# Sum of squares of a recurrence head as two rounded products, two key tiles later

## The chip, the cores and the metric

The kernel runs on one core of a Trainium2 chip. The metric is the device time of one execution in microseconds (us). Engines are called as the profile calls them: PE (TensorE matmul), PEld (its weight load), DVE (VectorE), ACT (ScalarE), POOL (GpSimd) and SP (SyncE, which here issues the loads of weights).

## The reference

Two blocks in a row work on x of 512 tokens and 1024 features: a gated MLP and a chunked attention, then a block with two branches, one of which is a gated linear recurrence with 8 heads of 128 channels. The change touches what follows the recurrence of a head: its output is divided by the root of its mean square over the 128 channels, and gated.

```python
    o = hgrn2_recurrence(q, k, v, log_f).astype(dt)
    o = rms_norm_2(o, hg_norm_g)          # per token, over the 128 channels of a head
    o = o * jax.nn.silu(hz).reshape(B, S, HG_HEADS, HG_DIM)
```

with `rms_norm_2(x, g) = x * rsqrt(mean(x*x) + 1e-6) * g`.

## The kernel before

Activations lie with features on the 128 partitions and the 512 tokens along the free axis. A product whose result must be near float32 is done as three products of rounded halves (`mm3`, lines 462 to 464): a tensor is cut into a high part (ACT, type fp32r) and the remainder (DVE or POOL, fp32r), and PE runs high by high, low by high, high by low. Weights come in 512 KB slabs: SP loads a slab into `raw` (L440), ACT rounds it (`whi`, L973, called `cut()`), POOL subtracts (`wlo`, L452), and PE's `slab()` multiplies it in 8 key tiles k = 0 to 7 with three products of 512 columns each.

The engines' programs are written out by hand and run in that order; semaphores (`Steps`, one count per named step) are the only link. The recurrence is a software pipeline over rounds r = 0 to 7. In round r PE runs the slabs `hq` r, `hf` r, `mz` r-2 and `hz` r, and between their key tiles it puts small products of head s = r-1: in slab `hq` (`hg_scores`, L737) the transposes of the keys after k = 3, the diagonal score blocks after k = 4 and 5, the cross blocks after k = 6 and 7; in slab `hf` (`hg_updates`, L750) the state updates after k = 3, 4 and 5, which wait for DVE's `ktlo` (L1773); in slab `hz` (`hg_outputs`, L761) the outputs, into bank 3. Slab `hq` also carries, after k = 2, the step that is changed, for head u = r-2: `hg_square` (L732) multiplies the all-ones matrix by the squared output `ho`, which gives each token's sum of squares on all partitions in bank 6. The square of head 6 stands in slab `dn` 0 in the same manner; that of head 7 stands alone behind slab `dn` 3 (L815).

ACT's round r (L1260 to 1299) is: `hg_root(u)` (square L1188, wait for the product, Ln L1190, Exp L1192), a cut, the two gates of `z`, the high part `kthi` of the transposed keys (L1209), a cut, the high part of the scores (L1216), Silu of the query (L1226), a cut that waits until PE has done slab `hf` r, then sigmoid and logarithm of the forget gate, the state halves, a cut, the exponentials (`hg_decays`) and four high parts (`hg_halves`, the last of them L1257). DVE's round is `hg_finish(u)` (L1760: norm, gate, `yhi`, `ylo`; it begins by waiting for ACT's Exp), `hg_stage(s)` (L1771) and `hg_project(r)` (L1797 to L1847), which ends with the low parts `klo`, `kolo`, `qlo` and `qblo` (L1839 to L1846). So PE in round r squares head r-2 when DVE is at the end of `hg_project(r-1)` or past it.

Of the kernel before, what the change touches and what calls it, by code (L numbers as in the profile page):

```python
# [22 lines left out]
F32 = mybir.dt.float32  # L23
F32R = mybir.dt.float32r
U32 = mybir.dt.uint32
ALU = mybir.AluOpType
ACT = mybir.ActivationFunctionType

P = 128
S = 512  # L30
# [8 lines left out]
HH = 8  # L39
# [93 lines left out]
def build(nc, xt, w, vecs, ws, bs, relx, consts, masks_hg, masks_ml, xs, rel_tab, tk, out):  # L133
    ctx = ExitStack()
    with ctx:
        def sb(name, shape, dt, where=ctx):
            return where.enter_context(nc.sbuf_tensor(name, shape, dt))

        def sem(name):
            return ctx.enter_context(nc.semaphore(name))  # L140
# [4 lines left out]
        ident, ones, eps = cst[:, 0:P], cst[:, P:2 * P], cst[:, 2 * P:2 * P + 1]  # L145
# [12 lines left out]
        yhi = sb("yhi", [P, AH, S], F32R)  # L158
# [5 lines left out]
        ylo = sb("ylo", [P, AH, S], F32R)  # L164
# [48 lines left out]
        with ExitStack() as scope:  # L213
            he = sb("he", [P, S], F32, scope)
            hf = sb("hf", [P, S], F32, scope)
            hk = sb("hk", [P, S], F32, scope)
            hb = sb("hb", [P, S], F32, scope)
            hd = sb("hd", [P, S], F32, scope)
            heb = sb("heb", [P, S], F32, scope)
            hen = sb("hen", [P, S], F32, scope)  # L220
            hq = sb("hq", [P, S], F32, scope)
            hx = sb("hx", [P, TT, 12], F32, scope)
            hfac = sb("hfac", [P, TT, 12], F32, scope)
            hqx = sb("hqx", [P, TT, HX], F32, scope)
            hqxs = [sb(n, [P, TT, HX], F32R, scope) for n in ("hqxhi", "hqxlo")]
            hqb = sb("hqb", [P, TT - 1, P], F32, scope)
            hqbs = [sb(n, [P, 2, TT - 1, P], F32R, scope) for n in ("hqbhi", "hqblo")]
            hks = [sb(n, [P, S], F32R, scope) for n in ("hkhi", "hklo")]
            hkos = [sb(n, [P, S], F32R, scope) for n in ("hkohi", "hkolo")]
            hkb = sb("hkb", [P, TT - 1, P], F32, scope)  # L230
            hkts = [sb(n, [P, TT - 1, P], F32R, scope) for n in ("hkthi", "hktlo")]
            hs = sb("hs", [P, S], F32, scope)
            hss = [sb(n, [P, S], F32R, scope) for n in ("hshi", "hslo")]
            hst = sb("hst", [P, TT - 1, P], F32, scope)
            hsts = [sb(n, [P, TT - 1, P], F32R, scope) for n in ("hsthi", "hstlo")]
            hz = sb("hz", [P, 2, S], F32, scope)
            ho = sb("ho", [P, 2, S], F32, scope)
            hm = sb("hm", [P, S + P + CROSS], F32, scope)
# [32 lines left out]
        bank = [banks[:, i * S:(i + 1) * S] for i in range(8)]  # L271
# [17 lines left out]
        def steps(name, names, rounds=1, prime=0):  # L289
            s = Steps(sem(name), names, rounds, prime)  # L290
            all_steps.append(s)
            return s
# [13 lines left out]
        def norm_steps(name, n, cut, squares=False):  # L306
            v = ["mean", "inv"]
            for t in range(n + 1):
                v += [f"full{t}"] if t < n else []
                if t >= 1:  # L310
# [25 lines left out]
                    for n in ("affine", "gate", "y", "yhi", "ylo")], 8, prime=1)  # L336
# [20 lines left out]
        hpV = steps("hp_dve", ["k", "b", "rest", "t12", "t03", "pairs", "mid", "three0", "three1", "four", "qin", "kin",  # L357
                               "kout", "two", "three", "kb", "qb", "klo", "kolo", "qlo", "qblo"], HH)
# [1 line left out]
        htA = steps("ht_act", ["z", "kthi", "shi", "sthi"], HH)  # L360
        htV = steps("ht_dve", ["ktlo", "diag", "near", "mid", "far", "slo", "st1", "st2", "st3", "stlo"], HH)
        hoP = steps("ho_pe", ["ms"], HH)
        hoA = steps("ho_act", ["sq", "ln", "root"], HH)
        hoV = steps("ho_dve", ["norm", "y", "yhi", "ylo"], HH)
        mzA = steps("mz_act", ["z"], HH)
        hzV = steps("hz_dve", ["zero", "one0", "one1"])
        dnP = steps("dn_pe", ["tok", "wide"])
        dnA = steps("dn_act", numbered("sq", QL + KL) + ["kp", "root", "wide0", "wide1"] + numbered("hi", QL + KL))
        dnV = steps("dn_dve", ["q1", "q2", "k1"] + ["turn"] + numbered("cross", 4) + ["sum", "mean", "inv", "kplo", "diag"]
# [31 lines left out]
        def f32(ap):  # L401
            return ap.bitcast(F32)
# [54 lines left out]
        def _(pe):  # L457
# [243 lines left out]
            def hg_keys(s):  # L701
                pe.wait_ge(hpV.sem, hpV.at("kb", s))
                if s >= 1:
                    pe.wait_ge(htV.sem, htV.at("st3", s - 1))
                for t in range(TT - 1):
                    last = nc.tensor.transpose(bank[4][:, t * P:(t + 1) * P], hkb[:, t, :], ident)
                last.then_inc(htP.did("kt"), 1)

            def hg_diagonal(s, t):
                if t == 0:  # L710
                    pe.wait_ge(hpV.sem, hpV.at("qlo", s))
                    if s >= 1:
                        pe.wait_ge(htV.sem, htV.at("diag", s - 1))
                cols = slice(t * P, (t + 1) * P)
                last = mm3(bank[5][:, cols], [u[:, cols] for u in hks], [u[:, t, 0:P] for u in hqxs], True, True)
                if t == TT - 1:
                    last.then_inc(htP.did("diag"), 1)

            def hg_cross(s, t):
                if t == 0:  # L720
                    if s >= 1:
                        pe.wait_ge(htV.sem, htV.at("far", s - 1))
                        pe.wait_ge(hoA.sem, hoA.at("ln", s - 1))
                if t == 2 and s >= 2:
                    pe.wait_ge(mzA.sem, mzA.at("z", s - 2))
                cols = slice(t * P, (t + 1) * P)
                last = mm3(banks[:, 6 * S + t * 2 * P:6 * S + t * 2 * P + CROSS], [u[:, cols] for u in hkos],
                           [u[:, t, HC:HX] for u in hqxs], True, True)
                if t == TT - 1:
                    last.then_inc(htP.did("cross"), 1)  # L730

            def hg_square(u):  # L732
                pe.wait_ge(hoA.sem, hoA.at("sq", u))
                pe.wait_ge(htV.sem, htV.at("far", u))
                nc.tensor.matmul(bank[6], ones, ho[:, 0, :], start=True, stop=True).then_inc(hoP.did("ms"), 1)  # L735

            def hg_scores(r, k):  # L737
                s, u = r - 1, r - 2
                if k == 2 and u >= 0:
                    hg_square(u)  # L740
                if k == 3:
                    hg_keys(s)
                if k in (4, 5):
                    hg_diagonal(s, 2 * (k - 4))
                    hg_diagonal(s, 2 * (k - 4) + 1)
                if k in (6, 7):
                    hg_cross(s, 2 * (k - 6))
                    hg_cross(s, 2 * (k - 6) + 1)
# [31 lines left out]
            for r in range(HH):  # L780
                s, u = r - 1, r - 2
# [111 lines left out]
            for g, t in enumerate((0, QL)):  # L893
                for b in range(TT):
                    tok = nc.tensor.matmul(bank[6][:, g * TT + b:g * TT + b + 1], dsq[:, t, b * P:(b + 1) * P], ones[:, 0:1],
                                           start=True, stop=True)
# [61 lines left out]
        def _(act):  # L958
# [57 lines left out]
            for r in range(4):  # L1016
                for j in range(4):
                    if r or j:
                        cut()
                    if r in (1, 2):  # L1020
                        k = 4 * (r - 1) + j
# [162 lines left out]
            def hg_root(u):  # L1184
                if u >= 1:
                    act.wait_ge(hoV.sem, hoV.at("ylo", u - 1))
                act.wait_ge(htP.sem, htP.at("o", u))
                nc.scalar.activation(ho[:, 0, :], bank[3], ACT.Square).then_inc(hoA.did("sq"), 1)  # L1188
                act.wait_ge(hoP.sem, hoP.at("ms", u))
                nc.scalar.activation(ho[:, 1, :], bank[6], ACT.Ln, bias=eps, scale=1.0 / P).then_inc(hoA.did("ln"), 1)  # L1190
                act.wait_ge(hoA.sem, hoA.at("ln", u))
                nc.scalar.activation(ho[:, 1, :], ho[:, 1, :], ACT.Exp, scale=-0.5).then_inc(hoA.did("root"), 1)  # L1192
# [67 lines left out]
            for r in range(HH + 1):  # L1260
                s, u = r - 1, r - 2
                if u >= 0:
                    hg_root(u)
# [156 lines left out]
        def _(dve):  # L1420
            V = nc.vector
# [36 lines left out]
            def cols(name, n, first=0):  # L1458
                return [vec[:, VEC[name] + first + t:VEC[name] + first + t + 1] for t in range(n)]
# [298 lines left out]
                return ap.to_broadcast([P, *shape])  # L1758

            def hg_finish(u):  # L1760
                dve.wait_ge(hoA.sem, hoA.at("root", u))
                V.scalar_tensor_tensor(ho[:, 0, :], bank[3], cols("hg_g", 1)[0], ho[:, 1, :], ALU.mult,
                                       ALU.mult).then_inc(hoV.did("norm"), 1)
                dve.wait_ge(hoV.sem, hoV.at("norm", u))
                V.tensor_tensor(ho[:, 0, :], ho[:, 0, :], hz[:, u % 2, :], ALU.mult).then_inc(hoV.did("y"), 1)
                dve.wait_ge(hoV.sem, hoV.at("y", u))
                V.tensor_copy(yhi[:, u, :], ho[:, 0, :]).then_inc(hoV.did("yhi"), 1)
                dve.wait_ge(hoV.sem, hoV.at("yhi", u))
                V.tensor_tensor(ylo[:, u, :], ho[:, 0, :], f32(yhi[:, u, :]), ALU.subtract).then_inc(hoV.did("ylo"), 1)
# [79 lines left out]
            V.memset(hs[:, :], 0.0).then_inc(hzV.did("zero"), 1)  # L1849
            V.memset(hfac[:, :, 0:1], 1.0).then_inc(hzV.did("one0"), 1)  # L1850
            V.memset(hfac[:, :, 11:12], 1.0).then_inc(hzV.did("one1"), 1)
            dve.wait_ge(st_x, 16)
            dve.wait_ge(ld_hm, 16)
            dve.wait_ge(hzV.sem, hzV.all())
# [254 lines left out]
```

## Time and profile before

| | us |
|---|---|
| three runs | 1358.9, 1359.68, 1362.27 (median 1359.68) |
| the profiled execution: its own time | 1360.59 |
| its span, first to last instruction | 1358.8 |
| PE busy in the span | 1306.7 (96%) |
| DVE, ACT, POOL busy | 719.0, 646.5, 493.8 |

The profile gives start and duration of each instruction. PE's instructions are pipelined, so a product of 512 columns is shown 0.39 us long while the next one starts 0.23 us after it: PE's work is read from the distance between starts and not from durations. The rounds of the recurrence lie between 700 and 1010 us and repeat every 29.6 us.

### The profile page before, as it was taken

What the parts mean: (1) busy time and instruction counts of PE and PEld (TensorE: products, weight loads), DVE (VectorE), ACT (ScalarE), POOL (GpSimd) and SP (SyncE); (2) the same over time, 40 slices, a digit from 0 to 9 for tenths busy, and PEclk for the clock granted to TensorE, in tenths of its full rate; (3) what the DMA queues carried; (4) which work ended last, traced back from release to release, by engine and by line L of the source; (5) the groups of instructions that cost most, each with busy time, mean ns of one, the idle gap of its engine ahead of it and who ended that gap; (6) DMA issues with size and microseconds to landing.
All of it is one profiled execution on the core that took longest, in us unless ns stands there. A gap on an engine that the chain in (4) does not pass through costs nothing.

```text
span 1358.8 us, 16181 instructions
## 1 busy us (share of the span) xinstructions
PE 1306.7 (96%) x6346; PEld 1084.1 (80%) x6346; DVE 719.0 (53%) x1256; ACT 646.5 (48%) x957; POOL 493.8 (36%) x206
## 2 busy tenths in 40 slices
PE   6999999999999999999998899999999999999985
PEld 4787888888888888888876788888887888888864
DVE  6464646552236465554766376766626546642325
ACT  4344444542334556464435466656546545542211
POOL 2454344434444323322334433333333333234430
PEclk9999999999999999999999999999999999999998
DMA  5542232334232322322224322222223222234421
GB/s 222 187 139 87 92 99 82 93 101 156 94 108 93 92 78 80 104 62 72 68 82 147 109 63 62 72 78 68 78 93 96 73 80 87 88 103 153 131 62 62
DMA packets 42155, 132.31 MB, mean 97 GB/s; under 512 B 6944, under 2 KB 9696, under 8 KB 41440
## 3 DMA queue, kind: packets, MB, share of 16 engines
q1 hardware_dynamic: 36704, 116.41, 27.2%
q10 hardware_dynamic: 5376, 14.87, 3.1%
q8 instruction: 50, 0.82, 0.2%
q14 instruction: 25, 0.20, 0.0%
HBM read 124.97 MB, written 10.49 MB: 100 GB/s over the span
## 4 chain that ended last, share of the span: by engine, by line
PE 78%; DVE 11%; ACT 6%; issue 2%; DMA 1%; POOL 1%; ACTq 0%; DVEq 0%; SPq 0%
PE banks L462 24%; PE banks L464 24%; PE banks L463 24%; DVE hd L1805 1%; PE banks L624 1%; PE banks L613 1%; DVE naccb L1705 1%; ACT L1232 1%; POOL wlo L452 1%; DVE hb L1802 1%; ACT L1233 1%; PE banks L856 1%; DVE acc L1478 1%; PE banks L735 1%; DMA x_kept<-x 1%
## 5 line engine op out<-in xcount | busy, mean ns | idle before, releaser
L452 POOL TENSOR_TENSOR wlo<-raw,whi 128x1024 fp32r<-128x1024 f32 (+2 forms) x202 | 493.6, 2446 | 829.8 <-ACT whi L973 829.8
L462 PE MATMUL banks<-hhi,whi 128*128 128x512 f32 x752 | 304.7, 405 | 4.5 <-POOL wlo L452 3.3
L973 ACT ACTIVATE whi<-raw 128x1024 fp32r<-128x1024 f32 (+2 forms) x202 | 210.2, 1041 | 201.8 <-PE banks L464 149.4
L464 PE MATMUL banks<-hlo,whi 128*128 128x512 f32 x752 | 294.3, 391 | 0.0
L463 PE MATMUL banks<-hhi,wlo 128*128 128x512 f32 x752 | 294.1, 391 | 0.0
L462 PE MATMUL banks<-yhi,whi 128*128 128x512 f32 x448 | 176.5, 394 | 0.0
L464 PE MATMUL banks<-ylo,whi 128*128 128x512 f32 x448 | 174.6, 390 | 0.0
L463 PE MATMUL banks<-yhi,wlo 128*128 128x512 f32 x448 | 174.4, 389 | 0.0
L462 PEld LDWEIGHTS banks<-hhi,whi 128*128 128x128 f32 x752 | 142.0, 189 | 33.2 <-issue 5.6
L464 PEld LDWEIGHTS banks<-hlo,whi 128*128 128x128 f32 x752 | 141.6, 188 | 30.6
L463 PEld LDWEIGHTS banks<-hhi,wlo 128*128 128x128 f32 x752 | 142.0, 189 | 26.8 <-issue 1.9
L462 PE MATMUL banks<-whi,yhi 128*128 128x512 f32 x224 | 90.4, 404 | 18.0 <-DVE ylo L1470 12.3
L462 PEld LDWEIGHTS banks<-yhi,whi 128*128 128x128 f32 x448 | 84.1, 188 | 20.8 <-issue 3.0
L464 PEld LDWEIGHTS banks<-ylo,whi 128*128 128x128 f32 x448 | 84.1, 188 | 17.9
L463 PEld LDWEIGHTS banks<-yhi,wlo 128*128 128x128 f32 x448 | 84.2, 188 | 17.0
L463 PE MATMUL banks<-whi,ylo 128*128 128x512 f32 x224 | 88.6, 396 | 0.0
L464 PE MATMUL banks<-wlo,yhi 128*128 128x512 f32 x224 | 88.4, 395 | 0.0
L462 PEld LDWEIGHTS banks<-whi,yhi 128*128 128x128 f32 x224 | 42.8, 191 | 29.0 <-POOL wlo L452 19.2
L1107 ACT ACTIVATE sc<-sc,sm 128x128 f32<-128x128 f32 (+1 forms) x64 | 35.1, 553 | 47.2 <-DVE sm L1664 47.2
L463 PEld LDWEIGHTS banks<-whi,ylo 128*128 128x128 f32 x224 | 42.9, 192 | 9.5 <-issue 0.7
L464 PEld LDWEIGHTS banks<-wlo,yhi 128*128 128x128 f32 x224 | 42.9, 192 | 9.1
L1557 DVE SCALAR_TENSOR_TENSOR mt<-banks,vec,bb 128x512 f32<-128x512 f32 x16 | 12.0, 751 | 70.0 <-PE banks L554 70.0
(359 smaller groups left out, 2116.1 us busy)
## 6 DMA issues: line engine op xcount, KB each, us to landing
raw<-w SPq DMA_DIRECT2D x194, 512.0 KB, 3.5
rel_tab<-relx ACTq DMA_DIRECT2D x1, 4096.0 KB, 21.4
tab<-rel_tab SPq DMA_DIRECT2D x16, 224.0 KB, 3.5
x<-xt SPq DMA_DIRECT2D x4, 512.0 KB, 6.5
x<-xt ACTq DMA_DIRECT2D x1, 2048.0 KB, 8.1
x_kept<-x ACTq DMA_DIRECT2D x1, 2048.0 KB, 7.3
parts_kept<-mcg SPq DMA_DIRECT2D x8, 256.0 KB, 4.4
mgt<-parts_kept SPq DMA_DIRECT2D x8, 256.0 KB, 3.9
```

Of the source, the lines that this page charges most:

```text
L452: nc.gpsimd.tensor_tensor(wlo[:, n % 4, 0:width], raw[:, n % 2, 0:width], f32(whi[:, n % 4, 0:width]), ALU.subtract).then_inc(lo_done, 1)
L462: nc.tensor.matmul(dst, a[0], b[0], start=first, stop=False)
L463: nc.tensor.matmul(dst, a[1], b[0], start=False, stop=False)
L464: return nc.tensor.matmul(dst, a[0], b[1], start=False, stop=last)
L613: done = nc.tensor.matmul(banks[:, c:c + QW[t]], a[rows, t * P:(t + 1) * P], b[rows, 0:QW[t]], start=first, stop=last)
L624: last = nc.tensor.transpose(banks[:, c:c + P], sc[:, q, of:of + P], ident)
L735: nc.tensor.matmul(bank[6], ones, ho[:, 0, :], start=True, stop=True).then_inc(hoP.did("ms"), 1)
L856: last = nc.tensor.transpose(bank[b][:, c:c + P], msc[:, QO[t] + k * P:QO[t] + (k + 1) * P], ident)
L973: nc.scalar.activation(whi[:, n % 4, 0:width], raw[:, n % 2, 0:width], ACT.Copy).then_inc(hi_done, 1)
L1107: e = nc.scalar.activation(row, row, ACT.Exp, bias=sm[:, q, 1, t:t + 1], accum_out=sm[:, q, 2, t:t + 1])
L1232: nc.scalar.activation(he[:, :], bank[0], ACT.Sigmoid).then_inc(hpA.did("f"), 1)
L1233: act.preload_act_table_set("natural_log_exp_and_others")
```

## The change

The ones matrix is copied once to a rounded tile `hones`. ACT, right behind the square, writes its high part `hsqhi`; DVE subtracts and writes the low part `hsqlo` at the head of `hg_finish(u)`; PE multiplies `hones` by both parts, in fp32r, and does so after key tile 4 instead of 2, ahead of the diagonal blocks. `hsqhi` has the place of `hq`, `hsqlo` that of `heb`, in the buffer.

```diff
-            heb = sb("heb", [P, S], F32, scope)
+            with ExitStack() as place:
+                heb = sb("heb", [P, S], F32, place)
+            hsqlo = sb("hsqlo", [P, S], F32R, scope)
...
-            hq = sb("hq", [P, S], F32, scope)
+            with ExitStack() as place:
+                hq = sb("hq", [P, S], F32, place)
+            hsqhi = sb("hsqhi", [P, S], F32R, scope)
+            hones = sb("hones", [P, P], F32R, scope)
...
             def hg_square(u):
-                pe.wait_ge(hoA.sem, hoA.at("sq", u))
+                pe.wait_ge(hoV.sem, hoV.at("sqlo", u))
                 pe.wait_ge(htV.sem, htV.at("far", u))
-                nc.tensor.matmul(bank[6], ones, ho[:, 0, :], start=True, stop=True).then_inc(hoP.did("ms"), 1)
+                nc.tensor.matmul(bank[6], hones[:, :], hsqhi[:, :], start=True, stop=False)
+                nc.tensor.matmul(bank[6], hones[:, :], hsqlo[:, :], start=False, stop=True).then_inc(hoP.did("ms"), 1)
...
-                if k == 2 and u >= 0:
+                if k == 4 and u >= 0:
                     hg_square(u)
...
                 nc.scalar.activation(ho[:, 0, :], bank[3], ACT.Square).then_inc(hoA.did("sq"), 1)
+                act.wait_ge(hoA.sem, hoA.at("sq", u))
+                act.wait_ge(hpV.sem, hpV.at("qin", min(u + 1, HH - 1)))
+                nc.scalar.activation(hsqhi[:, :], ho[:, 0, :], ACT.Copy).then_inc(hoA.did("sqhi"), 1)
                 act.wait_ge(hoP.sem, hoP.at("ms", u))
...
             def hg_finish(u):
+                dve.wait_ge(hoA.sem, hoA.at("sqhi", u))
+                V.tensor_tensor(hsqlo[:, :], ho[:, 0, :], f32(hsqhi[:, :]), ALU.subtract).then_inc(hoV.did("sqlo"), 1)
                 dve.wait_ge(hoA.sem, hoA.at("root", u))
...
             V.memset(hfac[:, :, 11:12], 1.0).then_inc(hzV.did("one1"), 1)
+            V.tensor_copy(hones[:, :], ones).then_inc(hzV.did("ones"), 1)
```

## Rows read from the trace of the kernel before

**Rows 1.** The page: busy time of the engines, share of the span, instructions (part 1)

```profile
PE 1306.7 (96%) x6346; PEld 1084.1 (80%) x6346; DVE 719.0 (53%) x1256; ACT 646.5 (48%) x957; POOL 493.8 (36%) x206
```

**Rows 2.** PE's waits, 785 to 1000 us: engine, line, releaser, total us, times, longest

```profile
PE banks L735 <- ACT ho L1188: 1.2, 6, 0.4
```

**Rows 3.** Timeline of PE around one square: start, duration (us), engine, line, operation, tiles

```profile
844.38 0.39 PE L464 MATMUL banks<-hlo,whi 128*128 128x512 f32 x1
844.91 1.12 PE L735 MATMUL banks<-ho,cst 128*128 128x512 f32 x2
...
846.10 0.39 PE L463 MATMUL banks<-hhi,wlo 128*128 128x512 f32 x1
...
847.59 0.23 PE L462 MATMUL banks<-hqxhi,hkhi 128*128 128x128 f32 x1
```

**Rows 4.** Timeline of DVE in the same stretch

```profile
843.26 0.55 DVE L1835 TENSOR_TENSOR hqb<-hqx,hfac 128x384 f32<-128x384 f32 x1
843.73 0.69 DVE L1839 TENSOR_TENSOR hklo<-hen,hkhi 128x512 fp32r<-128x512 f32 x1
...
845.93 0.56 DVE L1846 TENSOR_TENSOR hqblo<-hqb,hqbhi 128x384 fp32r<-128x384 f32 x1
```

**Rows 5.** Timeline of ACT in the same stretch and behind it

```profile
844.28 0.58 ACT L1188 ACTIVATE ho<-banks 128x512 f32<-128x512 f32 x1
846.07 0.69 ACT L1190 ACTIVATE ho<-banks,cst 128x512 f32<-128x512 f32 x1 [1.22 <-PE banks L735]
...
850.66 0.49 ACT L1209 ACTIVATE hkthi<-banks 128x384 fp32r<-128x384 f32 x1
852.21 1.06 ACT L973 ACTIVATE whi<-raw 128x1024 fp32r<-128x1024 f32 x1 [1.05 <-PE banks L464]
```

**Rows 6.** Timeline of PE around the square of head 7, which waits for nothing

```profile
996.17 1.02 PE L735 MATMUL banks<-ho,cst 128*128 128x512 f32 x2
...
997.27 0.40 PE L463 MATMUL banks<-hhi,wlo 128*128 128x512 f32 x1
```

**Rows 7.** Timeline of PE: rounded products of 512 columns behind a wait

```profile
44.95 0.50 PE L462 MATMUL banks<-whi,yhi 128*128 128x512 f32 x1 [3.02 <-POOL wlo L452]
45.29 0.40 PE L463 MATMUL banks<-whi,ylo 128*128 128x512 f32 x1
45.53 0.40 PE L464 MATMUL banks<-wlo,yhi 128*128 128x512 f32 x1
```

**Rows 8.** Timeline, one product of PE that waits for DVE

```profile
777.79 0.56 DVE L1794 TENSOR_TENSOR hstlo<-hst,hsthi 128x384 fp32r<-128x384 f32 x1 [5.97 <-ACT hsthi L1220]
...
778.41 0.33 PE L462 MATMUL banks<-hqbhi,hsthi 128*128 128x128 f32 x1 [2.91 <-DVE hstlo L1794]
```

**Rows 9.** Timeline of ACT, the cut that waits for slab `hf`

```profile
859.12 1.06 ACT L973 ACTIVATE whi<-raw 128x1024 fp32r<-128x1024 f32 x1 [3.10 <-PE banks L464]
```

**Rows 10.** Timeline, DVE's `ktlo` and the state update of PE that waits for it

```profile
852.12 0.55 DVE L1773 TENSOR_TENSOR hktlo<-banks,hkthi 128x384 fp32r<-128x384 f32 x1
...
855.10 0.22 PE L462 MATMUL banks<-yhi,hkthi 128*128 128x128 f32 x1
```

**Rows 11.** Timeline of POOL, from 840 to 856 us (in brackets: idle before)

```profile
848.46 2.73 POOL L452 TENSOR_TENSOR wlo<-raw,whi 128x1024 fp32r<-128x1024 f32 x1 [9.06 <-ACT whi L973]
853.35 2.41 POOL L452 TENSOR_TENSOR wlo<-raw,whi 128x1024 fp32r<-128x1024 f32 x1 [2.16 <-ACT whi L973]
```

**Rows 12.** DVE's line 1805: count, duration in ns (min/median/max), first and last start

```profile
L1805 DVE TENSOR_TENSOR hd<-hb x8: 691/2703/2716, 738.2 to 955.8; 128x512 f32<-128x512 f32 x8
```

**Rows 13.** Timeline, a DVE subtraction from a PSUM bank beside POOL

```profile
611.88 2.37 POOL L452 TENSOR_TENSOR wlo<-raw,whi 128x1024 fp32r<-128x1024 f32 x1 [12.73 <-ACT whi L973]
612.79 0.69 DVE L1634 TENSOR_TENSOR klo<-banks,khi 128x512 fp32r<-128x512 f32 x1 [3.76 <-ACT khi L1091]
```

**Rows 14.** Timeline of DVE, its first instruction of the recurrence behind the memsets

```profile
734.90 0.68 DVE L1799 TENSOR_SCALAR hk<-he,lbn,lb 128x512 f32<-128x512 f32 x1 [10.38 <-ACT he L1232]
```

**Rows 15.** Stretch 785 to 1000: busy us (instructions) of PE, PEld, DVE, ACT, POOL; clock, DMA

```profile
785.00:1000.00 215.00, 213.63 (x1117) 178.31 (x1116) 134.83 (x229) 126.03 (x175) 74.80 (x28) 1.00 0.22 69
```

More of the change, by code:

```diff
@@ L362, in build @@
         hoP = steps("ho_pe", ["ms"], HH)
-        hoA = steps("ho_act", ["sq", "ln", "root"], HH)
-        hoV = steps("ho_dve", ["norm", "y", "yhi", "ylo"], HH)
+        hoA = steps("ho_act", ["sq", "sqhi", "ln", "root"], HH)
+        hoV = steps("ho_dve", ["sqlo", "norm", "y", "yhi", "ylo"], HH)
         mzA = steps("mz_act", ["z"], HH)
-        hzV = steps("hz_dve", ["zero", "one0", "one1"])
+        hzV = steps("hz_dve", ["zero", "one0", "one1", "ones"])
         dnP = steps("dn_pe", ["tok", "wide"])
```

## Prediction

> **What bounds the kernel now.** I read the page first: PE is busy 96% of the span, the next engine 53% [rows 1]. Between 785 and 1000 us, where all eight squares lie, PE is busy 213.6 of 215.0 us at a granted clock of 1.00 [rows 15]. So a microsecond taken off PE's own sequence there is worth one, and a wait put into it costs one. Then PE's waits: in that stretch the list has one entry, the square itself, for ACT's square [rows 2]. Its 1.2 us are too small a reading, since idle time is counted there from the modelled end of a product; from start to start, as below, the wait is longer. Last, the timelines of PE, DVE and ACT around one square, that of head 2 at 844.9 us, on which all that follows is read; the other six squares inside a slab have the same distances within some 0.02 us, but for head 0, whose wait is longer.
>
> **What a square costs today.** The last product of key tile 2 starts at 844.38 [rows 3]; at 0.23 us a product its place ends at 844.61. The square starts at 844.91, when ACT's square (844.28 + 0.58 = 844.86) is there [rows 5]: a wait of 0.30. The next slab product but one starts at 846.10, so key tile 3 begins at 846.10 - 0.23 = 845.87, and the square took 0.96 us. Key tile 3, the transposes and key tile 4 take until the first diagonal product at 847.59, which is 1.72 us. Altogether 844.61 to 847.59 is 0.30 + 0.96 + 1.72 = 2.98 us. The square of head 7 waits for nothing: 996.17 to 997.27 - 0.23 = 997.04, 0.87 us [rows 6].
>
> **What it costs after, part by part.** The wait for ACT's square goes, and PE does the same 1.72 us of tiles first. It asks for `sqlo` at 844.61 + 1.72 = 846.33.
>
> When is `sqlo` ready? ACT's new copy to `hsqhi` has the size of the high parts beside it, some 0.63 us, starts at 844.9 and is done by about 845.5. Its wait for `qin` costs nothing, since DVE has passed L1819 long before L1835 at 843.26 [rows 4]. But DVE is in order, and `sqlo` stands behind the whole of `hg_project`. Its last instruction, `qblo`, starts at 845.93; behind one of that size the next starts 0.47 us later (843.26 to 843.73), thus at 846.40, and a subtraction of 128x512 with two SBUF inputs takes 0.69: 847.09 [rows 4]. From DVE's end to PE's start it is 0.06 us (777.79 + 0.56 = 778.35, to 778.41) [rows 8]. So PE goes on at 847.15: it waits 0.82 us where it waited 0.30. Nothing but PE's own stream is queued behind this wait, and on DVE nothing: it would have waited for ACT's Exp anyway.
>
> The pair itself: the trace before has no such pair, but has rounded products of 512 columns behind a wait, 44.95 to 45.29 (0.34) and then 0.24 a product [rows 7]; with 0.23 for the second it is 0.57. The first diagonal product starts at 847.15 + 0.57 = 847.72, against 847.59. Each square inside a slab costs **0.13 us more**: the 0.39 saved in the product and the 0.30 of the old wait are taken by the new wait.
>
> Is this distance kept from round to round? DVE's `hg_project` is not paced by the squares but by the slab `hf`: ACT's cut waits 3.10 us for that slab to end [rows 9], and sigmoid, logarithm, scan, exponentials and halves follow in a fixed chain down to `qblo` (from 859.12 to one round of 29.6 us behind 845.93, at 875.5, it is 16.4 us). PE runs without a wait from `hf`'s end to the next square. So PE and DVE meet with the same distances each round, and the 0.13 us are added each time. Head 0 has the same distance from `qblo` to the diagonal, the 1.66 us from 845.93 to 847.59 [rows 3, 4], and only the waits before and after are longer there, by equal amounts.
>
> Seven squares give 7 x 0.13 = +0.9 us. The square of head 7 comes a whole slab after ACT's square, with DVE idle, so both parts are there when PE asks at 996.17: 0.46 for 0.87 [rows 6], -0.4 us. **Sum +0.5 us.**
>
> *What is moved.* Ln can start at 847.15 + 0.34 + 0.39 + 0.04 = 847.92 instead of 846.07 [rows 5], so the whole chain of Ln, Exp, a cut, `kthi`, norm, `yhi`, `ylo` and `ktlo` comes 1.85 us later. Its cover: `ktlo` ends at 852.67 and PE's update starts at 855.10 [rows 10], 2.43 us; after, 854.52 against 855.23, so 0.7 us are left. The cross blocks, which must wait for Ln to have read bank 6, start two key tiles (1.4 us) and four blocks after the first diagonal product, so behind 849.1, and Ln is done by 848.61. ACT's idle 3.10 before the cut of `hf` shrinks to about 1.25 [rows 9] and still lets the chain start on time. The cuts of this part serve slabs that PE needs a slab or more later. All this costs nothing while those gaps stand.
>
> *The copy of the ones* is one DVE instruction (smaller than the 0.69 us of a 128x512 subtraction, or up to the 2.7 of one held by POOL [rows 4, 12]) ahead of 10.38 us in which DVE is idle [rows 14]: nothing.
>
> *Bounds.* `sqlo` 0.69 to 0.75 and its start 0.47 to 0.60 behind `qblo`; the way to PE 0.05 to 0.10; the pair 0.46, as with hidden loads, to 0.67, with a first product as slow as a half of today's square behind its wait. The diagonal then comes 1.58 to 2.12 us behind 845.93, against 1.66: -0.08 to +0.46 a head, with the last head -1.0 to +2.8 us in sum. I take the middle rows, as they are of the same shapes.
>
> On contention with POOL: line 1805 takes 691 ns alone and 2703 ns at the median, when it meets POOL's subtraction [rows 12]. `hsqlo` would be exposed in the same way; POOL, though, is idle for the 9.06 us before 848.46 [rows 11], and `sqlo` lies at 846.4 to 847.1. The Trainium skill (SBUF — State Buffer, "Who interferes with whom") says that a DVE instruction with two SBUF inputs contends with a GpSimd instruction that reads SBUF, whoever is second being fully blocked. By that rule the new subtraction can be held, unlike one that reads a bank; the trace agrees in the 2.0 us of line 1805.
>
> **The rivals.**
>
> *Faster: the new wait isn't there.* If `sqlo` were ready by the time PE asks, each of seven squares would save 0.30 + 0.96 - 0.46 = 0.80, with the last 6.0 us: 1353.7. For it: this is what two more key tiles of distance look like from ACT's side alone, as `hsqhi` is ready 0.8 us before PE asks. Against it: DVE's order; it would have to finish `qblo` 0.8 us earlier, and nothing in the change shortens that chain. Each 0.1 us that the wait is shorter gives 0.7.
>
> *Slower: the later root makes `ktlo` late.* `kthi` comes at 850.66 + 1.85 and ends at 853.0, ACT's cut, which today waits for PE until 852.21, then starts behind it, and POOL's subtraction starts 1.14 later, at about 854.1, within 0.2 us of `ktlo` at 853.97 [rows 5, 10, 11]. If POOL held `ktlo` as it holds line 1805, `ktlo` would end at 854.1 + 2.4 + 0.55 = 857.05, PE would wait 1.9 us in each of seven slabs `hf`, and the time be 13 us more: 1373. Against it: `ktlo` reads a PSUM bank and one SBUF tile, and such a subtraction in the midst of POOL's takes 0.69, its usual time [rows 13]. It decides from a delay of the root of 2.43 + 0.13 us on, whatever its cause.
>
> *Slower: `sqlo` meets POOL.* 2.0 us in each of seven squares, 14 us, 1374; it needs a POOL subtraction in a gap of 9 us where there is none now.
>
> **How the numbers follow.** The sum is made against the profiled execution: 1360.59 us, span 1358.8; it lies 0.9 above the median of the three runs, inside their 1358.9 to 1362.27. +0.5 on it gives 1361.1, on the median 1360.2; I predict for the median. The forecast (a change between -1.0 and +2.8) has 0.83; faster by the missing wait 0.06; slower by `ktlo` 0.06; by `sqlo` and POOL 0.03; 0.02 is left for a gain in between. For the range: the bounds give 1358.7 to 1362.5, and medians of this kernel spread by about a microsecond beside; 1357.0 to 1363.3 leaves out the three rivals and some of the rest. What a measurement can tell from no change is 0.3%, 4.1 us, so the forecast and its bounds lie within: same 0.83, faster 0.08, slower 0.09.
>
> **What would show it.** In the profile after, for each of seven squares: the first of the pair starts 1.2 us after `qblo`'s start, PE waits for DVE's `sqlo` some 0.8 us from start to start (0.6 by the list of waits, which counts from modelled ends), the diagonal starts 1.79 us after `qblo`'s start instead of 1.66; the rounds repeat every 29.7 to 29.8 us; POOL doesn't touch `sqlo`, which takes 0.69; `ktlo` ends 0.7 us before the update, and PE's list shows no wait for it. Head 7's square takes 0.46. The prediction is wrong if `qblo` ends earlier against PE than before, if `ktlo` appears in the list, or if PE's products outside the squares change their distance.

## Result and profile after

| | before | after |
|---|---|---|
| median of six runs each (us) | 1361.41 | 1366.86 |
| ratio of the runs | | 1.0049, 95% interval 1.0036 to 1.0061 |
| span of the profiled execution | 1358.8 | 1365.8 |

The change makes the kernel slower by 0.49%, some 6.7 us by the ratio (4.9 to 8.3 by its interval; the two medians differ by 5.5); the prediction was 0.5 us slower, in a range that ended at 1363.3. The time of this kernel scatters by 3 to 4 us from run to run and more over a long series, so each experiment is compared with runs of the kernel before on the same chip. A ratio below is a kernel's time over that of the kernel before, with its 95% interval in brackets; a time in us beside it is the ratio times the kernel before.

PE's waits between 785 and 1000 us, the view of [rows 2] (engine, line, what it waited for, total us, times, longest), show two entries, neither of them the one of before:

```profile
PE banks L467 <- ACT mzg L1212: 4.2, 6, 0.7
PE banks L740 <- DVE hsqlo L1771: 4.0, 6, 0.7
```

The second was forecast. The first was not in the prediction at all. It is PE waiting for ACT's Silu of the slab `mz` (L1203 of the kernel before, written to `mzg`), which empties bank 7. It is called the gate below.

PE's timeline around the square of head 2 answers to [rows 3]; lines 467 to 469 are now the three products of `mm3`:

```profile
848.80 0.40 PE L469 MATMUL banks<-hlo,whi 128*128 128x512 f32 x1
849.86 0.50 PE L740 MATMUL banks<-hsqhi,hones 128*128 128x512 f32 x1 [0.66 <-DVE hsqlo L1771]
850.20 0.40 PE L741 MATMUL banks<-hsqlo,hones 128*128 128x512 f32 x1
850.43 0.22 PE L467 MATMUL banks<-hqxhi,hkhi 128*128 128x128 f32 x1
...
853.16 0.25 PE L467 MATMUL banks<-hqxhi,hkohi 128*128 128x192 f32 x1
...
853.47 0.27 PE L467 MATMUL banks<-hqxhi,hkohi 128*128 128x192 f32 x1
...
854.31 0.40 PE L469 MATMUL banks<-hlo,whi 128*128 128x512 f32 x1
855.38 0.36 PE L467 MATMUL banks<-hqxhi,hkohi 128*128 128x192 f32 x1 [0.68 <-ACT mzg L1212]
...
855.80 0.27 PE L467 MATMUL banks<-hqxhi,hkohi 128*128 128x192 f32 x1
```

The last product of key tile 4 starts at 848.80, its place ends at 849.03, and the pair starts at 849.86: a wait of 0.83 us. The pair is 0.34 + 0.23. Then the four cross blocks: the third, which writes bank 7, should follow key tile 7 at 854.54 and starts at 855.38, 0.84 us late; the fourth comes 0.42 instead of 0.31 behind it.

DVE's and ACT's timelines of the same stretch answer to [rows 4] and [rows 5]:

```profile
848.65 0.55 DVE L1857 TENSOR_TENSOR hqblo<-hqb,hqbhi 128x384 fp32r<-128x384 f32 x1
849.12 0.68 DVE L1771 TENSOR_TENSOR hsqlo<-ho,hsqhi 128x512 fp32r<-128x512 f32 x1
```

```profile
846.99 0.58 ACT L1194 ACTIVATE ho<-banks 128x512 f32<-128x512 f32 x1
847.61 0.63 ACT L1197 ACTIVATE hsqhi<-ho 128x512 fp32r<-128x512 f32 x1
850.63 0.69 ACT L1199 ACTIVATE ho<-banks,cst 128x512 f32<-128x512 f32 x1 [2.40 <-PE banks L741]
851.35 0.63 ACT L1201 ACTIVATE ho<-ho 128x512 f32<-128x512 f32 x1
851.89 1.04 ACT L979 ACTIVATE whi<-raw 128x1024 fp32r<-128x1024 f32 x1
852.95 1.28 ACT L1207 ACT_TABLE_LOAD   x1
854.25 0.60 ACT L1207 ACTIVATE hz<-banks 128x512 f32<-128x512 f32 x1
854.74 0.59 ACT L1212 ACTIVATE mzg<-banks 128x512 f32<-128x512 f32 x1
```

The last fence has the whole path: the product of PE releases Ln, and Exp, the cut, a table load and the Silu of `hz` stand between it and `mzg`, which ends at 855.33, 0.05 us before PE goes on. In the kernel before, the same instruction of ACT and the same cross block of PE lay like this:

```profile
850.19 0.59 ACT L1203 ACTIVATE mzg<-banks 128x512 f32<-128x512 f32 x1
851.68 0.25 PE L462 MATMUL banks<-hqxhi,hkohi 128*128 128x192 f32 x1
```

The gate ended at 850.78 and PE came at 851.68: 0.9 us to spare, which a chain 1.85 us later uses up.

The wait is in the code of the kernel before: `hg_cross` (L719) waits, at its third block and from head 2 on, for `mzA.at("z", s - 2)`.

### The profile page after: what moved, and what is told of

It is laid out like the page before. It is cut to its first block, busy times and chain, and to the rows that moved or that the text cites. A ratio compares the mean times of both kernels' runs of the same rounds, so it can differ in the third digit from the quotient of the medians.

```text
span 1365.8 us, 16206 instructions
## 1 busy us (share of the span) xinstructions
PE 1307.3 (96%) x6346; PEld 1086.0 (80%) x6346; DVE 723.3 (53%) x1265; ACT 650.3 (48%) x965; POOL 493.4 (36%) x206
## 4 chain that ended last, share of the span: by engine, by line
PE 76%; DVE 13%; ACT 6%; issue 3%; DMA 1%; POOL 1%; ACTq 0%; DVEq 0%; SPq 0%
PE banks L467 24%; PE banks L469 23%; PE banks L468 23%; DVE hd L1816 1%; PE banks L629 1%; PE banks L618 1%; DVE naccb L1714 1%; ACT whi L979 1%; ACT L1241 1%; POOL wlo L457 1%; ACT L1242 1%; PE banks L862 1%; DVE acc L1487 1%; DVE hb L1813 1%; ACT L1207 1%
## 5 line engine op out<-in xcount | busy, mean ns | idle before, releaser
L467 PE MATMUL banks<-whi,yhi 128*128 128x512 f32 x224 | 90.5, 404 | 18.1 <-DVE ylo L1479 12.5
```

Of the source, the lines that this page charges most:

```text
L467: nc.tensor.matmul(dst, a[0], b[0], start=first, stop=False)
```

## Experiments

Theory A was that the loss is the wait for the gate, set by how late the square's product is *for ACT*, and that the meeting of PE and DVE at `hsqlo` costs what was forecast. Theory B was that something else at the square, or the clock, is the loss.

**The gate alone, in the kernel before.** Extra copies on ACT behind Exp delay ACT's chain and leave PE's and DVE's programs as they are:

```diff
                 nc.scalar.activation(ho[:, 1, :], ho[:, 1, :], ACT.Exp, scale=-0.5).then_inc(hoA.did("root"), 1)
+                act.wait_ge(hpV.sem, hpV.at("qin", min(u + 1, HH - 1)))
+                for i in range(n):
+                    if i:
+                        act.wait_ge(hoA.sem, hoA.at("pad" + str(i - 1), u))
+                    nc.scalar.activation(hq[:, :], heb[:, :], ACT.Copy).then_inc(hoA.did("pad" + str(i)), 1)
```

With n = 1:

> The kernel before with one extra copy of 128x512 on ACT behind Exp: ACT's chain 0.6 us later, less than the 0.85 us that the gate mzg has to spare. Theory A: no wait for mzg, no change within 1 us. A theory in which each delay of ACT's chain costs PE time: +3.6 us.

Measured: ratio 1.0006 (0.9995 to 1.0018). PE's list has no wait for `mzg`. With n = 3:

> The kernel before with three extra copies of 128x512 on ACT behind Exp, which move only ACT's own chain by some 1.9 us; PE, DVE's norm and the square are as before. Theory A: the gate has 0.85 us to spare, so PE waits 1.05 + 0.11 us in each of six rounds: +7 us, and the wait for mzg stands in PE's list. Theory B (the gate is not what PE's time hangs on): no change.

Measured: ratio 1.0069 (1.0052 to 1.0086), some 9 us (7.1 to 11.7). PE's waits, 785 to 1000 us:

```profile
PE banks L462 <- ACT mzg L1208: 4.9, 6, 0.8
PE banks L735 <- ACT ho L1188: 0.5, 1, 0.5
```

The rounds are 30.70 us long (from `qblo` to `qblo`, mean of five), against 29.64 in the kernel before: 1.06 a round, where 1.16 was expected. The copies behind the square of head 7 add one more wait of 1.0 us for the gate, at 1011 us, which the expectation had left out. Together this is some 7.4 us, at the lower end of the interval; the runs don't show what the rest is. One delay below the 0.9 us to spare costs nothing and one beyond it costs the excess, and the changed kernel lies beyond it.

**The gate relieved, in the changed kernel**, once from ACT's side and once from PE's. ACT's cut behind the gates:

```diff
-                cut()
                 if s >= 0:
                     hg_silu_z(s)
                 if r >= 3:
                     ml_silu_z(r - 3)
+                cut()
```

> The changed kernel with ACT's cut between Exp and the two gates of z put behind the gates, nothing else. Theory A (the loss is PE's wait, in the cross blocks after key tile 7, for ACT's gate mzg, which frees bank 7): the gate comes 1.05 us earlier against a wait of 0.84, the wait disappears from the list and 6 x 0.96 us come back; what is left against the kernel before is 7 x 0.12 - 0.41 = +0.4 us, so within 1 us of it. Theory B (the loss comes from DVE's and PE's new meeting at the square, or from the clock after the wait at 778 us): the time stays some 6 us above the kernel before.

Measured: ratio 0.9998 (0.9989 to 1.0007). PE's waits, 785 to 1000 us:

```profile
PE banks L740 <- DVE hsqlo L1771: 4.0, 6, 0.7
```

And the two blocks that need bank 7 later in PE's order:

```diff
-                if k in (6, 7):
-                    hg_cross(s, 2 * (k - 6))
-                    hg_cross(s, 2 * (k - 6) + 1)
+                if k == 6:
+                    hg_cross(s, 0)
+                    hg_cross(s, 1)
...
             def hg_updates(s, k):
+                if k == 1:
+                    hg_cross(s, 2)
+                    hg_cross(s, 3)
```

> The changed kernel with the last two cross blocks, the ones that write bank 7, moved from behind key tile 7 of slab hq to behind key tile 1 of the next slab, 1.4 us later in PE's order; ACT is as in the changed kernel. Theory A (PE waits for the gate): the wait disappears, within 1 us of the kernel before. Theory B: stays 6 us above. If DVE's copies of the cross blocks were what is late next, the state updates would show a wait for ktlo, or slab mz for the scores.

Measured: ratio 1.0005 (0.9995 to 1.0015), the same single entry of 4.0 us in the list, and rounds of 29.77 us in both, +0.13 against the kernel before. So with the gate out of the way the change is what was forecast: no difference that can be measured. Theory B falls.

**Each half of the change alone.** The move without the rounding (in the kernel before, `if k == 2` becomes `if k == 4`):

> The kernel before with the float32 square at key tile 4 instead of 2, no rounding. Theory A: no wait for ACT's square (saves 0.30 a head and the exposed load, 0.39 together), Ln 1.3 us later, gate at 852.15 against a PE that asks at 851.3: a wait of 0.85 and 0.11 behind it. Net +0.57 in six heads, -0.39 in one: +3.0 us. Theory B (only the new wait for DVE costs): -0.39 x 7 = -2.7 us.

Measured: ratio 1.0031 (1.0017 to 1.0044), 4.2 us (2.3 to 6.0) where 3.0 was expected, rounds of 30.16 us, +0.52 against an expected 0.57:

```profile
PE banks L462 <- ACT mzg L1203: 4.1, 6, 0.7
```

So it is the move that brings the wait for the gate, with or without the new instructions. The rounding without the move (in the changed kernel `if k == 4` becomes `if k == 2`):

> The changed kernel with the square put back behind key tile 2: rounding without the move. Theory A (PE meets DVE at the end of its projection step wherever it asks earlier): PE asks at 844.61 and gets the low part at 847.15, a wait of 2.5 us, pair 0.57, then 1.72 of tiles: the first diagonal product 3.5 us behind the start of qblo against 1.66, +1.85 in each of seven heads, with the last -0.4: +12.5 us. The gate is as late against PE as it was before, so no wait for mzg. Theory B (the pair or DVE's order costs nothing, only the gate does): about -3 us.

Measured: ratio 1.0142 (1.0118 to 1.0166), 19 us. There is no wait for `mzg`, and seven waits for `hsqlo`, 16.9 us together:

```profile
PE banks L740 <- DVE hsqlo L1771: 16.9, 7, 2.7
```

From `qblo` to `qblo` the six rounds are 32.8, 33.1, 31.5, 33.1, 31.5 and 33.1 us long: two of them are +1.86, as expected, and four are longer. The difference is the clock. PE's timeline in one of the long rounds, and busy time and granted clock (the value behind the five engines) of stretches around it:

```profile
821.99 0.50 PE L740 MATMUL banks<-hsqhi,hones 128*128 128x512 f32 x1 [2.37 <-DVE hsqlo L1771]
...
823.66 0.84 PE L711 MATMUL banks<-cst,hkb 128*128 128x128 f32 x3
824.15 0.77 PE L467 MATMUL banks<-hhi,whi 128*128 128x512 f32 x1
```

```profile
819.00:822.00 3.00, 0.63 (x4) 0.20 (x2) 2.93 (x5) 1.33 (x3) 0.00 (x0) 1.00 0.00 0
822.00:825.00 3.00, 3.00 (x10) 2.45 (x11) 0.83 (x2) 2.21 (x3) 0.00 (x0) 0.62 0.00 0
```

PE has stood idle for 2.4 us here, and the granted clock of the next 3 us is 0.62 on average, a mix of 2.4 GHz and the lower level of 1.2 GHz; such a round is 1.57 us longer, the first of the four, which has a wait of 2.7 us, 1.3. The expectation of 12.5 us had left this out; with the four it is 18.5 us.

**Further from its input, and slower.** The changed kernel with `if k == 5`:

> The changed kernel with the square behind key tile 5 instead of 4, nothing else. Theory A: the wait for hsqlo goes (PE asks at 847.7, it is there at 847.1), and the gate, whose chain hangs on the square, is 0.4 us later still while PE asks 1.3 earlier: a wait for mzg of 2.2 + 0.1 us in each of six rounds, rounds of 31.1 us, +7 us against the kernel before. Moving the square further from its input makes it slower. A theory by which the wait for hsqlo was the loss: -6 us.

Measured: ratio 1.0081 (1.0055 to 1.0107), rounds of 31.13 us, +1.49:

```profile
PE banks L467 <- ACT mzg L1212: 12.4, 6, 2.1
PE banks L467 <- DVE hktlo L1784: 0.5, 1, 0.5
```

The wait for `hsqlo` is gone and the kernel is 11 us slower than before, as it must be if the gate sets the time and not the wait for `hsqlo`. One of its rounds is 32.7 us long, with a mean clock of 0.95 from 941 to 975 us and 1.00 on both sides of it; this and the clock at 778 us (below) are likely the rest from 7 to 11 us.

**Toward a faster kernel.** What is left with the gate relieved is the wait of 0.83 us for `hsqlo`. Taking it before `qblo`, with ACT's cut as in `cut_later` (`hg_square_lo` is the wait for `sqhi` and the subtraction, taken out of `hg_finish`):

```diff
                 V.tensor_tensor(hqxs[1][:, :, :], hqx[:, :, :], f32(hqxs[0][:, :, :]),
                                 ALU.subtract).then_inc(hpV.did("qlo"), 1)
+                if r >= 1:
+                    hg_square_lo(r - 1)
                 dve.wait_ge(hpA.sem, hpA.at("qbhi", r))
```

> The changed kernel with two edits: ACT's cut behind the gates, as in cut_later, and DVE's low part hsqlo taken ahead of qblo instead of behind it. PE waits for hsqlo from 846.33 to 846.68 by the rows of before, pair 0.57, first diagonal product 1.32 us behind the place of qblo's start today against 1.66: -0.34 in seven heads, -0.4 for head 7 and -0.5 at the norm factors behind it: -3.3 us against the kernel before, if Theory A (gate and DVE's order are the two costs) holds. Theory B: no better than cut_later.

Measured: ratio 0.9982 (0.9967 to 0.9997), -2.4 us. The wait is 1.7 us in seven times by the list, rounds are 29.27 us, -0.37 for an expected -0.34. And the square at key tile 5 with both reliefs of the gate:

> The changed kernel with the square behind key tile 5, ACT's cut behind the gates, and the last two cross blocks behind key tile 1 of the next slab. By Theory A PE asks for hsqlo after it is there, the wait is gone, and each of seven heads saves 0.30 + 0.96 - 0.46 = 0.80: -6.5 us with the last, if ktlo, which has 0.3 us left by this count, is not late; if it is, some tenths of a us in each of seven slabs hf come back, and PE's list names ktlo.

Measured: ratio 0.9977 (0.9966 to 0.9988), -3.1 us, half of the -6.5; the rounds are some 29.4 us and one 30.1, not 28.8. What is late next is neither `hsqlo` nor `ktlo`. From the waits of 785 to 1000 us:

```profile
ACT whi L982 <- DMA raw<-w: 13.2, 7, 2.4
...
PE banks L467 <- DVE hqxlo L1857: 2.2, 5, 1.0
```

The cut that was put behind the gates also releases POOL's subtraction, and this the buffer of the next load but one: ACT's cut at slab `hf` now waits 2.4 us for the DMA where it waited for PE, and the chain to `qlo` starts late. So the place of the cut was the likely fault, and ACT has a better one, ahead of Ln, where it idles for PE's product:

```diff
                 nc.scalar.activation(hsqhi[:, :], ho[:, 0, :], ACT.Copy).then_inc(hoA.did("sqhi"), 1)
+                if u < HH - 1:
+                    cut()
                 act.wait_ge(hoP.sem, hoP.at("ms", u))
...
                 if u >= 0:
                     hg_root(u)
-                cut()
+                else:
+                    cut()
```

This edit alone in the changed kernel:

> The changed kernel with the one edit of the cut put between the copy to hsqhi and Ln; square at key tile 4, cross blocks as in the changed kernel. Theory A: the gate is 1.05 us earlier, no wait for mzg, the wait for hsqlo of 0.8 stays, rounds of 29.75 us, +0.4 us against the kernel before. If POOL, which now starts near 846.7, held hsqlo or what stands ahead of it, hsqlo would take up to 2.7 and PE wait up to 2 us longer in each of seven heads.

Measured: ratio 1.0002 (0.9989 to 1.0015), rounds of 29.74 us, `hsqlo` 0.68 to 0.69 us long, no wait for `mzg`. And with key tile 5 and the later cross blocks, which is the kernel of `k5_both` with the cut in this place:

> The changed kernel with the square behind key tile 5, the last two cross blocks behind key tile 1 of the next slab, and ACT's cut put between the copy to hsqhi and Ln, where ACT waits for the product anyway. In k5_both the cut stood behind the gates and the load of the slab after it came late: ACT's cut at slab hf waited for the DMA (13.2 us in seven rounds), the chain to qlo started late and PE waited for hqxlo. Theory A: with the cut ahead of Ln the load is early, that wait of ACT goes back to one for PE, PE waits for nothing in the rounds, which repeat every 28.8 us against 29.6: -6.5 us against the kernel before. If instead DVE's chain to qlo is the bound whatever the load does, the rounds stay at 29.3 and the gain at -3.

Measured: ratio 0.9951 (0.9932 to 0.9971), median 1353.96 us beside 1360.86 for the kernel before: **-6.7 us for an expected -6.5**, rounds of 28.82 us. So the place of the cut was the fault of `k5_both`. PE's list has no entry between 785 and 1000 us, and PE is busy in all of it (the row of [rows 15], of this kernel):

```profile
785.00:1000.00 215.00, 215.00 (x1144) 183.29 (x1143) 128.07 (x240) 133.68 (x186) 78.88 (x30) 1.00 0.23 69
```

This is about what the prediction had given its faster rival, 6.0 us, in which PE waits for nothing at the square.

## Why the prediction was wrong

**What held.** The meeting of PE and DVE: the first diagonal product was forecast 1.79 us behind the start of `qblo` and lies at 850.43 - 848.65 = 1.78; the wait for `hsqlo` 0.82, measured 0.83; the pair 0.57, measured 0.57; `hsqlo` at 0.69, measured 0.68, untouched by POOL. Head 7's square costs 0.47 (1004.21 to 1004.68), where 0.46 was forecast and it was 0.87. DVE's chain to `qblo` stays tied to slab `hf`: in `cut_later` and `cross_later`, where nothing else interferes, the rounds are 0.13 us longer, as forecast. The later root costs `ktlo` nothing: it ends at 857.20, 1.7 us before the update at 858.91, more than the 0.7 forecast only because PE is late itself. Neither slower rival came: POOL did not hold `ktlo` or `hsqlo`. For `ktlo` a trace shows the meeting itself: in `early_cut` it starts at 853.04, inside POOL's two subtractions from 852.71 to 857.47, and takes 0.56.

**What failed** is the step "What is moved". It followed the later root to `ktlo`, to the cross blocks' bank 6 and to the cuts, and said that all this costs nothing while those gaps stand; the step before it had said that nothing but PE's own stream is queued behind the new wait, but ACT's whole chain is. It named the instructions between Ln and `kthi` only as "a cut", and so left out the two Silus, `hz` and `mzg`, that stand between them, and who waits for each. The second, `mzg`, empties bank 7, and the third cross block writes that bank. Its gap was 0.9 us (850.78 to 851.68), the smallest that I find on this chain, and the root came 1.85 us later with PE only 0.13 later. Worked out in the manner of the other steps it gives 1.85 + 0.05 - 0.9 - 0.13 = 0.87 of wait and 0.11 for the exposed load behind it, six times, 5.9 us. Measured: 0.84 and 0.11, six times 0.95, 5.7 us. This term is what the sum lacked: 0.9 for seven squares, +5.7, -0.4 for head 7 and -0.5 at the norm factors behind it (PE's wait for `ddiag` at 1020 us was 1.2 and is 0.7) make 5.7, against a measured 6.7 with an interval of 4.9 to 8.3.

The trace of before had the gap in it. PE's list of waits held one entry, and the prediction asked of no other wait of PE's on this chain but those for `ktlo` and for Ln; a list of waits shows which gaps are negative, not which are small. The range was wrong for the same reason: its bounds were those of the costs that had been named, and a waiter that nobody had named had no chance of its own (the last 0.02 was for a gain in between). Its lower bound was also added wrongly: 0.47 + 0.69 + 0.05 + 0.46 is 1.67 us from `qblo` to the diagonal and not 1.58, so +0.01 a head and -0.3 in sum instead of -1.0. This changes nothing of the miss, which lies at the other end.

**The clock, in the profiled execution alone.** The span grew by 7.0 us, not 5.7. In both kernels PE waits 2.9 us for `hstlo` at 778 us. What follows differs. The rows of 778 to 784 us, first of the kernel before, then of the changed one:

```profile
778.00:784.00 6.00, 5.59 (x32) 4.91 (x33) 5.97 (x18) 3.25 (x7) 0.00 (x0) 1.00 0.12 47
```

```profile
778.00:784.00 6.00, 5.47 (x17) 4.73 (x18) 5.97 (x17) 3.12 (x7) 0.00 (x0) 0.50 0.14 55
```

The granted clock stayed at 2.4 GHz in the one and was 1.2 GHz in the other, 17 products against 32 in the same time. PE lost 2.7 us there and got 1.1 back, because its next stop, the square of head 0, needs no wait when PE comes later: the first diagonal product behind that square is 1.5 us later where 0.13 was forecast. The same wait of 2.9 us stands in the other traces, and the fall of the clock behind it doesn't follow the change: it fell in `pad1`, which is the kernel before with one copy more (0.68 in the 5 us behind the wait), in `cut_later`, `cross_later`, `fill` and `k5_alone` (0.66 to 0.68) and in `k5_both` (0.50), and did not in `pad3`, `move_alone`, `early_cut`, `k5_fill` and `round_alone` (1.00). With the two kernels above it fell in 7 of 13 profiled executions. It is scatter, and likely a part of what the time of this kernel varies by.

## What to carry to other kernels

When a step moves later, list every wait on every semaphore that its engine and the engines behind it will give later, with the gap of each, before calling a chain covered; the smallest gap decides, and a list of waits doesn't show it. A second use of an in-order engine (here a weight cut ahead of a gate) is often best placed where that engine idles for another one, and not where it merely is out of the way: the same cut behind the gates cost half of the gain through a late load. And putting a step further from its input helps only if what depends on its output is not nearer than the distance that it was moved.

## What the runs showed of the hardware

PE's clock fell from 2.4 to 1.2 GHz behind some of its idle times and not behind others of the same length: behind 2.4 us at three of six squares of `round_alone` (and behind the 2.7 us at the one before them), in one of the six rounds of `k5_alone` with a wait of 2.1 us, behind the 2.9 us at 778 us in 7 of 13 executions, and never in these traces behind the 0.8 us of the changed kernel. A fall in the rounds cost 1.3 to 1.6 us, the one at 778 us in the changed kernel 2.7. A product behind a wait took 0.11 us more than one that follows another: 0.34 instead of 0.23 for 512 columns, and 0.42 instead of 0.31 from the third to the fourth cross block.
